# Two transformer blocks on one core: where memory's values are projected, and which projections open the program

## What is computed

```python
# first block
xn = rms_norm(h, norm_mix_g)
sb_q, sb_k, sb_v, r_q, r_k, r_v, r_g = split(xn @ w_in)     # 512 columns each for sb_*
...                                                         # stick-breaking attention, retention, gates, w_out
hn = rms_norm(h, norm_ffn_g)
h = h + moe(hn)          # 16 experts, 2 per token: (silu(hn @ gate) * (hn @ up)) @ down, weighted
h = rms_norm(h, norm_final_g)
# second block
...                                                         # sparse and dilated attention
m = rmsnorm(mem, norm_mem_g)                                # memory: 256 tokens
k_mem, v_mem = split(m @ w_kv_cross)                        # 1024 columns each
...                                                         # cross attention on k_mem, v_mem; MLP
```

## Time and profile before

| what | value |
|---|---|
| median of three runs | 1719.45 us |
| profiled execution | 1720.16 us, span 1718.3 us |
| TensorE, VectorE, ScalarE, GpSimd busy | 1634.2, 937.8, 745.6, 608.5 us |
| mean granted TensorE clock | 0.983 of full |
| instructions | 21081 |
| DMA | 250.30 MB, mean 146 GB/s |

### The profile page before, as it was taken

The page is one execution under the profiler, slowest core; times in us unless marked ns, Lnnn a source line. Parts: engine busy times, 40 slices in busy tenths (PEclk is TensorE's granted clock), DMA queues, the critical chain, the costliest instruction groups (busy, mean ns, idle before and its releaser), DMA issues.

```text
span 1718.3 us, 21081 instructions
## 1 busy us (share of the span) xinstructions
PE 1634.2 (95%) x8000; PEld 1327.9 (77%) x8000; DVE 937.8 (55%) x1122; ACT 745.6 (43%) x895; POOL 608.5 (35%) x255
## 2 busy tenths in 40 slices
PE   8999999899999899999968989899999999999996
PEld 8888888658886878888857858766886888888885
DVE  6524310377174589999966679894433553231414
ACT  6344413234334577888854142475324322222221
POOL 1332154313434122232222616564431444444441
PEclk9999999999999999999989989999999999999998
DMA  7321034312223699999963314300321222222221
GB/s 260 125 74 50 25 111 133 112 37 98 98 103 112 233 414 421 404 389 390 393 244 119 103 49 139 110 1 1 132 89 50 93 79 100 96 98 98 98 98 49
DMA packets 46739, 250.30 MB, mean 146 GB/s; under 512 B 9456, under 2 KB 10224, under 8 KB 19920
## 3 DMA queue, kind: packets, MB, share of 16 engines
q1 hardware_dynamic: 40912, 238.89, 37.3%
q0 software_dynamic: 5184, 8.40, 1.4%
q10 hardware_dynamic: 576, 2.10, 0.3%
HBM read 239.20 MB, written 14.68 MB: 148 GB/s over the span
## 4 chain that ended last, share of the span: by engine, by line
PE 72%; issue 11%; DVE 7%; POOL 3%; DMA 3%; ACT 2%; SPq 1%; ACTq 0%; DVEq 0%; POOLq 0%
PE psum L229 21%; PE psum L231 20%; PE psum L230 20%; POOL w_lo L148 3%; PE psum L2175 2%; PE psum L2208 1%; DVE kept_bias L2062 1%; PE psum L718 1%; DVE top L2061 1%; PE psum L2196 1%; PE psum L2442 1%; DVE kept_bias L2054 1%; PE psum L1284 1%; ACT w_hi L142 1%; PE psum L737 1%
## 5 line engine op out<-in xcount | busy, mean ns | idle before, releaser
L148 POOL TENSOR_TENSOR w_lo<-raw,w_hi 128x2048 fp32r<-128x2048 f32 x93 | 428.4, 4606 | 739.8 <-ACT w_hi L142 704.5
L229 PE MATMUL psum<-x_hi,w_hi 128*128 128x512 f32 x840 | 330.1, 393 | 6.3 <-DVE w_lo L148 4.8
L230 PE MATMUL psum<-x_lo,w_hi 128*128 128x512 f32 x840 | 327.8, 390 | 0.0
L231 PE MATMUL psum<-x_hi,w_lo 128*128 128x512 f32 x840 | 327.8, 390 | 0.0
L142 ACT ACTIVATE w_hi<-raw 128x2048 fp32r<-128x2048 f32 x100 | 190.9, 1910 | 314.8 <-PE psum L231 311.0
L1302 DVE TENSOR_TENSOR moe_lo<-moe_w,moe_hi 128x2048 fp32r<-128x2048 f32 x99 | 225.7, 2290 | 37.0 <-ACT moe_hi L1292 35.1
L1292 ACT ACTIVATE moe_hi<-moe_w 128x2048 fp32r<-128x2048 f32 x99 | 189.3, 1915 | 36.8 <-PE psum L231 19.7
L229 PEld LDWEIGHTS psum<-x_hi,w_hi 128*128 128x128 f32 x840 | 158.3, 188 | 42.0 <-DVE w_lo L148 5.2
L230 PEld LDWEIGHTS psum<-x_lo,w_hi 128*128 128x128 f32 x840 | 158.3, 188 | 33.4 <-issue 0.7
L231 PEld LDWEIGHTS psum<-x_hi,w_lo 128*128 128x128 f32 x840 | 158.2, 188 | 33.1
L432 DVE TENSOR_TENSOR res<-res,psum 128x512 f32<-128x512 f32 x56 | 38.4, 687 | 217.6 <-PE psum L231 217.6
(11 more groups left out here) (370 smaller groups left out, 2889.0 us busy)
## 6 DMA issues: line engine op xcount, KB each, us to landing
raw<-in_w_dense SPq DMA_DIRECT2D x101, 1024.0 KB, 4.8
moe_w<-in_w_moe_ahead SPq DMA_DIRECT2D x54, 1024.0 KB, 14.6
moe_w<-in_w_moe SPq DMA_DIRECT2D x48, 1024.0 KB, 14.1
yrow<-expert_rows SPq DMA_DIRECT2D x8, 512.0 KB, 7.1
res<-in_x SPq DMA_DIRECT2D x4, 512.0 KB, 9.0
decay<-in_decay SPq DMA_DIRECT2D x8, 256.0 KB, 3.8
hn_rows<-hn_tok ACTq DMA_DIRECT2D x4, 512.0 KB, 4.6
out<-res SPq DMA_DIRECT2D x4, 512.0 KB, 2.6
```

The lines of the kernel that those rows point to most:

```text
L148: pool.tensor_tensor(w_lo[c % RING][:, :], raw[c % RING][:, :], w_hi[c % RING][:, :].bitcast(F32), ALU.subtract).then_inc(lo_ready, 1)
L229: pe.matmul(out, lh, rh, start=first, stop=False)
L230: pe.matmul(out, lh, rl, start=False, stop=False)
L231: return pe.matmul(out, ll, rh, start=False, stop=last)
```

## The change

v_mem leaves the head. The program starts with sb_q and sb_k, both from x times gain without the norm; VectorE evacuates both with the norm's factor. x's first quarter is loaded ahead of the first chunk. Of v_mem's inputs, the normed memory in high and low parts is stored to HBM when k_mem no longer delays the queue (two stores behind the layer "out"). Its four weight chunks are made a ninth entry of w_moe_ahead, so that the last turn loads them (and two of zeros) where it loaded pair 0's. Behind the loop ScalarE and VectorE split the fourth; SP brings the stored rows back into the buffers of chunks 6 and 7. TensorE makes six of the eight tiles before the combine's first transposes and two ahead of the third block; ScalarE evacuates them between its steps of the combine and issues the two stores of v_mem. The sums of squares come one block later. The factor by row in cross attention and its making go. At the routing, the split of expert chunk 2 stands behind k_mem's last evacuations.

```diff
-LAYERS = [("v_mem", 4), ("sb_q", 2), ("sb_k", 2), ("sb_v", 2), ("ret_v", 4), ("ret_q", 2), ("ret_k", 2),
+LAYERS = [("sb_q", 2), ("sb_k", 2), ("sb_v", 2), ("ret_v", 4), ("ret_q", 2), ("ret_k", 2),
...
     def norm_qkv_sync(sp):
         sp.dma_start(cols[:, :], d["cols"]).then_inc(cols_landed, 16)
-        sp.dma_start(mem0[:, :, :], d["mem"]).then_inc(mv_landed, 16)
-        load_chunk(sp, 0)
+        for g in range(4):
+            if g == 1:
+                load_chunk(sp, 0)
+            sp.dma_start(res[:, 2 * g:2 * g + 2, :], d["x"][:, 2 * g:2 * g + 2, :]).then_inc(x_landed[g], 16)
         load_chunk(sp, 1)
-        for g in range(4):
-            if g == 2:
-                load_chunk(sp, 2)
-            sp.dma_start(res[:, 2 * g:2 * g + 2, :], d["x"][:, 2 * g:2 * g + 2, :]).then_inc(x_landed[g], 16)
+        load_chunk(sp, 2)
         for name, tile in CONSTS:
             sp.dma_start(tile[:, :], d[name]).then_inc(consts_landed, 16)
         load_chunk(sp, 3)
-        dense_sync(sp, "v_mem")
-        sp.wait_ge(bank_free, FIRST_TILE["v_mem"] + KT + 4)
-        sp.dma_start(vc_rows, vc_out[:, :, :]).then_inc(v_moved, 16)
         for name in ("sb_q", "sb_k", "sb_v"):
             dense_sync(sp, name)
...
-        pool.wait_ge(lo_ready, 4)
-        split_lo(pool, 4)
-        split_lo(pool, 5)
+        pool.wait_ge(lo_ready, 2)
...
+        def key(j):
+            dve.wait_ge(tile_done, FIRST_TILE["sb_k"] + j + 1)
+            dve.tensor_tensor(sb_k[:, j, :], psum[:, (FIRST_TILE["sb_k"] + j) % 4, :], norm1.rstd[:, :], ALU.mult)\
+               .then_inc(bank_free, 1)
         x_low(0)
         x_low(1)
-        norm1.add_square(dve, 2)
+        first_low(0, first_high_done, first_low_done)
         x_low(2)
-        split_lo(dve, 2)
-        norm1.add_square(dve, 3)
         x_low(3)
-        norm1.add_square(dve, 4)
-        x_low(4)
-        split_lo(dve, 3)
+        first_low(1, hi_ready, lo_ready)
+        for kt in range(4, KT):
+            x_low(kt)
+        for kt in range(1, 5):
+            norm1.add_square(dve, kt)
+        split_lo(dve, 1)
         for kt in range(5, KT):
             norm1.add_square(dve, kt)
-            x_low(kt)
         norm1.vector_invert(dve)
+        norm1.wait_inverted(dve)
+        dve.wait_ge(bank_free, 4)
+        for j in range(3):
+            query(j)
         for g in range(4):
             dve.wait_ge(x_landed[g], 16)
-        norm1.vector_split(dve, between=queries)
-        query(2)
-        query(3)
+        norm1.vector_split(dve, between=lambda kt: query(3) if kt == 4 else None)
+        for j in range(4):
+            key(j)
...
+        def x_high(kt):
             act.wait_ge(x_landed[kt // 2], 16)
             act.activation(u_hi[:, kt, :], res[:, kt, :], ACT.Copy, scale=col("mix", kt)).then_inc(u_high, 1)
         x_high(0)
         x_high(1)
+        act.wait_ge(raw_landed[0], 16)
+        first_high(0, first_high_done)
         x_high(2)
+        x_high(3)
+        first_high(1, hi_ready)
+        for kt in range(4, KT):
+            x_high(kt)
+        for kt in range(5):
+            norm1.square(act, kt)
+        split_hi(act, 1, 0)
+        for kt in range(5, KT):
+            norm1.square(act, kt)
         split_hi(act, 2, 2)
         norm1.act_root(act)
         for kt in range(3):
             norm_high(kt)
+        split_hi(act, 3, 4)
         for kt in range(3, KT):
             norm_high(kt)
+        dense_act(act, "sb_k")
...
         class FirstParts:
             def wait_split(self, pe, n):
-                pe.wait_ge(mv_low, n)
+                pe.wait_ge(u_low, n)
                 if n == 1:
-                    pe.wait_ge(v_first_low, 1)
+                    pe.wait_ge(first_low_done, 1)
                 if n == 5:
                     pe.wait_ge(lo_ready, 1)
-        dense_pe(pe, "v_mem", mv_hi, mv_lo, token_major=True, norm=FirstParts(), by_parts=True,
-                 hooks={3: lambda: norm1.pe(pe)})
-        dense_pe(pe, "sb_q", u_hi, u_lo, norm=Parts(u_low))
-        dense_pe(pe, "sb_k", x_hi, x_lo, norm=norm1)
-        dense_pe(pe, "sb_v", x_hi, x_lo, token_major=True)
+        dense_pe(pe, "sb_q", u_hi, u_lo, norm=FirstParts(), by_parts=True, tile_hooks={1: lambda: norm1.pe(pe)})
+        dense_pe(pe, "sb_k", u_hi, u_lo)
+        dense_pe(pe, "sb_v", x_hi, x_lo, token_major=True, norm=norm1)
...
+        norm_mem.wait_split(sp)
+        sp.dma_start(m_rows[0], m_high[:, :, :].bitcast(F32)).then_inc(m_stored, 16)
+        sp.dma_start(m_rows[1], m_low[:, :, :].bitcast(F32)).then_inc(m_stored, 16)
...
             moe_rows_high(act, 0, 0)
             moe_split_chunk(act, 0, 1)
-            moe_split_chunk(act, 0, 2)
...
+        moe_split_chunk(act, 0, 2)
         moe_rows_high(act, 0, 1)
...
+    V_CHUNKS = 4
+    vm_hi, vm_lo = (at(f"v_mem_in_{n}", 16 + 8 * i, [P, KT, MEM], FR) for i, n in enumerate(("hi", "lo")))
+    vc_out = [at(f"v_mem{m}", kb, [P, D]) for m, kb in enumerate((140, 92))]
+    vc_rows = nc.dram_tensor("v_mem_rows", [P, MEM // P, D], F32).ap()
+    vm_landed, v_done, v_read, v_moved = (sem("v_mem_" + n) for n in ("in_landed", "tiles", "read", "moved"))
+
     def moe_sync(sp):
+        n_rounds = rounds_of(sp)
         sp.wait_ge(kv_moved, 16)
-        sp.wait_ge(v_moved, 16)
+        sp.wait_ge(m_stored, 32)
         sp.wait_ge(credits, 1)
 
         def body(n, i, r):
...
                   .then_inc(moe_landed[s // 2], 16)
             for s in range(MOE_AHEAD):
                 sp.wait_ge(moe_used, MOE_RING * n + MOE_RING + s + 1)
-                sp.dma_start(ring[s][:, :], d["w_moe_ahead"][bass.ds(i, 1), s].rearrange("a p n -> p (a n)"))\
+                ahead = i + ((n + (4 * PAIRS + 1) - n_rounds * PAIRS) >> 5 & 1)
+                sp.dma_start(ring[s][:, :], d["w_moe_ahead"][bass.ds(ahead, 1), s].rearrange("a p n -> p (a n)"))\
                   .then_inc(moe_landed[s // 2], 16)
-        n_rounds = expert_loop(sp, body)
+        expert_loop(sp, body, n_rounds)
+        for t, rows in ((vm_hi, m_rows[0]), (vm_lo, m_rows[1])):
+            sp.wait_ge(moe_used, n_rounds * (MOE_RING * PAIRS) + 8)
+            sp.dma_start(t[:, :, :].bitcast(F32), rows).then_inc(vm_landed, 16)
         for s in range(MOE_AHEAD // 2):
             sp.wait_ge(moe_landed[s], n_rounds * (32 * PAIRS) + 32)
             sp.sem_inc(wait_seen, 1)
-        sp.wait_ge(moe_low, n_rounds * (MOE_RING * PAIRS) + 3)
+        sp.wait_ge(moe_low, n_rounds * (MOE_RING * PAIRS) + V_CHUNKS)
...
+        pe.wait_ge(tr_ev[1], rounds_read[0] * (2 * PAIRS) + 2)
+        pe.sem_inc(wait_seen, 1)
+        pe.wait_ge(vm_landed, 32)
+
+    def v_mem_tensor(pe, s):
+        pe.wait_ge(moe_low, rounds_read[0] * (MOE_RING * PAIRS) + s + 1)
+        wh, wl = (t[:, :].rearrange("p (m k n) -> p m k n", k=KT, n=P) for t in (ring_hi[s % MOE_HI], ring_lo[s]))
+        for m in range(MEM // P):
+            j = 2 * s + m
+            if j >= 2:
+                pe.wait_ge(v_read, j - 1)
+            for kt in range(KT):
+                mm = three_pass(pe, psum[:, 7 * (j % 2), 0:2 * P], vm_hi[:, kt, m * P:(m + 1) * P],
+                                vm_lo[:, kt, m * P:(m + 1) * P], wh[:, :, kt, :], wl[:, :, kt, :], kt == 0, kt == KT - 1)
+            mm.then_inc(v_done, 1)
...
-        expert_loop(act, body)
+        n_rounds = expert_loop(act, body)
+        moe_split_chunk(act, n_rounds * PAIRS, 3)
...
-    yrow = [[at(f"yrow{k}{q}", 144 + 4 * (4 * k + q), [P, D]) for q in range(TB)] for k in range(2)]
+        n_rounds = expert_loop(dve, body)
+        moe_low_chunk(dve, n_rounds * PAIRS, 3)
...
+        def v_mem_out(j):
+            s, m = j // 2, j % 2
+            act.wait_ge(v_done, j + 1)
+            act.activation(vc_out[m][:, 256 * s:256 * s + 256], psum[:, 7 * (j % 2), 0:256], ACT.Copy).then_inc(v_read, 1)
+        for j in range(3):
+            v_mem_out(j)
         gated(0)
+        v_mem_out(3)
         gated(1)
+        v_mem_out(4)
+        v_mem_out(5)
         squared(0)
+        gated(2)
+        v_mem_out(6)
+        v_mem_out(7)
         high(0)
-        gated(2)
+        act.wait_ge(v_read, 8)
+        for m in range(MEM // P):
+            act.dma_start(vc_rows[:, m, :], vc_out[m][:, :]).then_inc(v_moved, 16)
         squared(1)
...
+        for s in range(3):
+            v_mem_tensor(pe, s)
         pe.wait_ge(g_squared, 1)
         for n in range(2 * TB):
             q, half = n // 2, n % 2
+            if n == 4:
+                v_mem_tensor(pe, 3)
...
-            if half and q >= 1:
-                sums(q - 1)
+            if half and q >= 2:
+                sums(q - 2)
+        sums(TB - 2)
...
```

102 lines of the change are left out of this document (14 added, 88 removed).

## The result

The changed kernel takes 1701.29 us (median of 4 runs, 1700.10 to 1703.08), the kernel before, on the same chip, 1720.37: a ratio of 0.9889 with a 95% interval of 0.9873 to 0.9905, so 19.1 us less (16.3 to 21.8). The forecast was 20.5 less, at 1699.0; its range was 1694 to 1706. The profiled execution took 1703.08, with a span of 1701.3, at a mean granted clock of 0.984.

A forecast was written before the change was run, and what follows sets the result against it. TensorE, busy 95% of the span, bounds the kernel: its work plus holes. Head -26.8, rows stored 0, entry +0.4, combine +6.1 and small items -0.2 sum to -20.5: 1699.0 us median, 8 in 10 from 1694 to 1706.

The forecast's parts named there:

- The head: Program start to the last sb_v tile: without v_mem and with x loaded first, it ends near 79.1, -26.8 us.
- first product near 9.7: Head: x's first piece lands near 4.9, chunk 0 near 7.4, so TensorE's first real product comes near 9.7 us.
- Rows stored: 0: Two 1 MB stores of memory's rows on SP's queue before the experts' first loads: cost 0, bounds 0 to 5 us.
- rival 2: Stores of memory's rows delay expert loads and gather by 2 to 5 us; entry costs +3 to +5: 1702.5; chance 0.16.
- Experts' entry: +0.4: From routing into the experts: an earlier start is lost waiting for chunks 6 and 7; net +0.4, bounds -5.8 to +3.
- Lets TensorE start at about 588.7 + 1.2 = 589.9 instead of 594.1: Experts' entry: splitting chunk 2 after the last evacuations starts TensorE 4.2 us earlier, plus 1.6 from the full clock.
- The half pace: Experts' entry: after a 4.9 us hole before hid's transposes, the clock halves for some 3.6 us, costing 1.8.
- the register load that SP now does before its wait: Experts' entry: SP's register load, moved ahead of its wait, was credited with 0.8 us for chunks 6 and 7.
- The combine: Behind the experts: v_mem's 23.0 us of products partly fill 12.77 us of idling; keys start +6.1 us later.
- +7.3: A size set against the combine's loss; the prediction as given here does not contain it.
- The list: Combine: TensorE's sequence of v_mem tiles, transposes and sums, timed from 880.8 to the keys' start at 925.0 against 918.90.
- SP's table loads come 5 us later, TensorE's tiles 6, so nothing new there: Behind the combine: table loads and TensorE's tiles shift about equally, so no further cost was added.

The follow-up runs named there:

- e1: Changed kernel with the two stores of memory's split rows issued earlier, among the chunk loads of the layer ahead of k_mem: 1699.01 us.
- e2: Changed kernel with ScalarE's split of expert chunk 2 put back ahead of the last two evacuations of k_mem's tiles: 1702.65 us.
- e4: Changed kernel with SP's seven table loads behind the combine issued ahead of its last weight chunk load, which waits for GpSimd: 1698.82 us.
- e11: Kernel before the change, with the seven table loads put ahead of the chunk load that waits for GpSimd: 1715.59 us.
- e3: Changed kernel with only one eighth of v_mem's products kept, its loads, splits, evacuations and stores staying: 1701.80 us.

## Why the prediction was right

Forecast were 20.5 us less, measured were 19.1 between the medians and 17.0 between the two traces from which the terms are read; the changed kernel's profiled execution was the slowest of its four.

**The head, -26.8 forecast, -26.04 measured.** The mechanism held in each piece: the wait for the norm's sum at 22.96 (22.0 forecast), one stop of VectorE of 4.69 us, x_lo there at 47.3 (47), no wait of sb_v. Mis-sized was "first product near 9.7": it is 10.40, since x's first piece landed at 5.37 and chunk 0 at 7.93, for 4.9 and 7.4. The slack ahead of the norm's sum takes a part of such a delay up: in the second trace, with a granted clock of 0.83 over 10 to 20 us, TensorE does not wait at the sum and ends at 80.02 all the same.

**"Rows stored: 0" failed.** The reason given, that the first loads are used only from 581 on, looked at the loads behind the stores on SP's own queue. What they hit was ScalarE's queue: hn's first two stores ran beside them, expert chunks 0 to 2 waited for those, and hn's last two stores then ran beside the chunks (median of the four: 4.6 us to land before and 9.7 now). With them went the gather, 7.49 us behind the last issue before and 12.05 now. That is rival 2, "the stores are in the way", in the place and of the size it named; it had the expert loads and the gather later as well, but not that the loads would do part of the delaying. The Trainium skill (DMA: Bandwidth & Descriptors, queues, rings and completion order) has each DMA engine take turns between queues; hn's first two stores agree (3.4 and 2.9 us before, 9.2 and 8.8 while SP's two run), and so does e1 (5.1 and 4.6). What the stores cost in the whole time is less sure: moving them alone gave 2.3 to 4.5 us by the medians and nothing in the trace's entry.

**"Experts' entry: +0.4" failed in its first step.** "Lets TensorE start at about 588.7 + 1.2 = 589.9 instead of 594.1" did not come: counted from the head's end the experts start 3.56 us later than before, not 4.2 earlier, since the gather holds TensorE up ahead of k_mem's last tiles. What the term says of an early start, that it runs into the supply of chunks 6 and 7, is seen in e1: there they start 2.7 us earlier than before on the same count and then wait 6.03 us. Both terms together were given as +0.4 and measured +4.04, with the doubt named above; 1.49 of it is the clock ahead of hn's rows, which no term had. The half pace forecast behind the hole before hid's transposes came in one trace of the changed kernel and not in the other (0.66 and 1.00 over 590 to 595 us); both have it where it was not forecast, behind the gather's hole (0.50 and 0.66 over 560 to 565). Chunk 2's split, on which the term was built, turned out worth nothing that can be told with the gather late (e2). The 0.8 us for "the register load that SP now does before its wait" do not show: 7.80 us from store to chunk 6 against 7.73.

**The combine, +6.1 forecast, +2.95 measured.** TensorE did not wait for v_mem's rows, the clock stayed up, the tiles came 2.88 us apart from the first one on (evacuations at 862.35, 865.23, 868.11), and the first v_mem product starts 0.28 us behind the start of the experts' last (859.19, 858.91), where products within a tile are 0.23 apart: the loop's exit costs nothing that can be seen, and +7.3 is out. At the keys' first product the loss is 4.1 (901.51 - 855.28 against 918.90 - 876.74), at VectorE's first read of their sums 46.52 - 42.02 = 4.5. The list is 1.6 to 2.0 too long, 1.4 of it up to the fourth block's transposes (889.95, 30.7 us behind the experts' end and not 32.1). The step that failed is "SP's table loads come 5 us later, TensorE's tiles 6, so nothing new there". The tables were the bound there already, and c_kv behind them is 1.1 to 1.5 us less late than TensorE is. e4 and e11 show the gate; with it removed from both kernels the term is +4.4.

So the errors of the entry and of the combine, +3.6 and -3.15, nearly cancel, and that the sum comes within 1.4 us of the medians' difference is owed in part to that luck. What is left between forecast and traces, 3.5 us, is 0.5 of these two, 0.8 of the head, 0.5 of the loop and 1.7 of the rest, for which -0.2 was forecast.

## What to carry to other kernels

A transfer that is used late is not free early: look at what shares the DMA engines in its window on every queue, above all stores that a gather waits for. If a hole's removal moves nothing in the trace, look for the next wait in the same chain of transfers and remove both; and where the stretch varies by some us with equal code, do not count on one trace for what each is worth. A store can also delay by way of a third transfer, that waits for the one it slowed. Work that fills a hole is charged at the difference of two chains, TensorE's and the one beside it: 20 us of products cost 3.5 here, and the order of a few loads behind them 4.6.

## What the runs showed of the hardware

The time from issue to landing of one 1 MB store is not set by its bytes: k_mem's store took 6.3 (before), 7.2 (changed), 12.7 (e1) and 11.3 us (e3), the last with the same code up to there as the changed kernel and issued as far behind chunks 3 to 5; why it took longer is open. With that the entry differs by 6.5 us between two executions of equal code, 521.96 and 528.43, while the loop behind it, 8 pairs long, repeats within 0.8.

Two stores can delay a third that starts only after they have landed: memory's had landed at 539.8, and hn's last, issued at 544.15, took 10.6 us for 6.1, because the loads that wait for hn's first stores had moved beside it.

The clock did not fall with every hole. In the changed kernel's first trace TensorE's waits of 4.39 us (before 560.79) and 3.70 us (before 921.81) were followed by stretches at the lower level, 1.2 GHz, and the one of 2.24 us (before 590.47) was not; in the second trace of the same kernel that place too ran at 0.66 over 590 to 595 us. A wait of 1.49 us ahead of hn's sum, which every kernel has, was followed by 0.51 over 530 to 532 us in the changed kernel's first trace and by 1.00 in that of before. The rest of the program, the same work in all kernels, took 782.9 to 785.9 us with its stretches at the lower clock in different places.
